# Attention over banded and dilated keys: turning the probability tiles beyond eight through one PSUM bank, interleaved with the other eight

## The reference, cut to what matters

```python
# window: query block n (128 queries) sees blocks n-1, n, n+1 and 256 context keys
p = softmax(concat([q @ k_local + mask, q @ k_context, sink]))
y = p_local @ v_local + p_context @ v_context
# grid: rows of 64, a query sees 8 rows x 16 columns around it, plus the context, with a bias
p = softmax(concat([q @ k_local + bias, q @ k_context]))
# dilated: causal, three dilations (128,1), (512,4), (2048,16), mixed by their softmax sums
y = sum(w[c] * (softmax(q @ k[c]) @ v[c]) for c in range(3))
```

## Time and profile before

| what | value |
|---|---|
| executions | 2537.91, 2540.40, 3635.32 us (median 2540.4) |
| profiled execution | 2537.63 us |
| its span, first to last instruction | 2535.7 us |
| PE busy of the span | 98% |
| DVE busy | 60% |
| ACT busy | 31% |
| mean granted TensorE clock | 0.995 of full |

### The profile page before, as it was taken

How to read it: one execution, slowest core, us unless ns; L and a number is a source line. 1 busy time by engine, 2 the same in 40 slices (tenths; PEclk the granted TensorE clock), 3 DMA queues, 4 the chain that set the end, 5 groups by cost and what they waited for, 6 DMA issues and landing times.

```text
span 2535.7 us, 38631 instructions
## 1 busy us (share of the span) xinstructions
PE 2472.3 (98%) x14777; PEld 1820.8 (72%) x14777; DVE 1508.9 (60%) x3740; ACT 784.9 (31%) x1752; POOL 299.9 (12%) x487
## 2 busy tenths in 40 slices
PE   6999999999999999999999999999999999999999
PEld 3477688777788685566788776868578866546867
DVE  2358776699866663443453477757868684514554
ACT  2237511277721123332210066113312274121210
POOL 1101100000051000000043022310000002222000
PEclk9999999999999999999999999999999999999999
DMA  7031000022033221311001011523240105334321
GB/s 276 21 108 52 23 34 34 34 76 80 14 100 108 68 98 44 104 41 43 9 23 43 34 50 44 104 100 117 83 150 34 67 27 142 115 108 174 126 97 52
DMA packets 75096, 193.69 MB, mean 76 GB/s; under 512 B 7821, under 2 KB 10577, under 8 KB 73985
## 3 DMA queue, kind: packets, MB, share of 16 engines
q0 software_dynamic: 28688, 99.67, 12.6%
q1 hardware_dynamic: 45472, 91.16, 10.3%
q10 hardware_dynamic: 752, 0.38, 0.1%
HBM read 149.46 MB, written 42.07 MB: 76 GB/s over the span
## 4 chain that ended last, share of the span: by engine, by line
PE 92%; DVE 3%; ACT 2%; issue 2%; DMA 1%; ACTq 0%; DVEq 0%; POOL 0%
PE psum L1586 37%; PE psum L1950 11%; PE psum L1890 7%; PE psum L1993 5%; PE psum L1990 5%; PE psum L2083 4%; PE psum L1974 3%; PE psum L1967 3%; PE psum L1700 3%; PE psum L1811 3%; PE psum L1572 1%; PE psum L1553 1%; PE psum L2154 1%; PE psum L2172 1%; PE psum L2141 1%
## 5 line engine op out<-in xcount | busy, mean ns | idle before, releaser
L3546 ACT ACTIVATE RP<-RP,small 128x1280 f32<-128x1280 f32 (+11 forms) x274 | 252.8, 923 | 154.8 <-DVE small L3056 154.5
L1950 PE MATMUL psum<-RQ 64*128 64x256 f32 (+5 forms) x1344 | 293.3, 492 | 2.0 <-DVE small L3056 1.2
L3056 DVE CUSTOM_DVE_ANT_0 RP<-psum,small 128x512 f32<-128x512 f32 (+1 forms) x382 | 201.8, 574 | 107.4 <-PE psum L1974 86.5
L1890 PE MATMUL psum<-RW,hT 128*128 128x512 f32 (+3 forms) x608 | 217.1, 512 | 1.0 <-ACT hT L3275 1.0
L1950 PEld LDWEIGHTS psum<-RQ 64*128 64x128 f32 (+1 forms) x1344 | 148.4, 191 | 72.0 <-issue 41.5
L1890 PEld LDWEIGHTS psum<-RW,hT 128*128 128x128 f32 x608 | 128.5, 216 | 75.1 <-issue 57.4
L1586 PE MATMUL psum<-RW,hT 128*128 128x256 f32 x736 | 167.0, 379 | 0.0
L1993 PE MATMUL psum<-RQ,RP 128*128 128x128 f32 x1312 | 159.8, 276 | 0.5 <-ACT YR L3580 0.5
L1993 PEld LDWEIGHTS psum<-RQ,RP 128*128 128x128 f32 x1312 | 152.1, 192 | 5.3 <-issue 4.6
L1586 PEld LDWEIGHTS psum<-RW,hT 128*128 128x128 f32 x736 | 139.6, 190 | 21.7 <-issue 2.2
L1586 PE MATMUL psum<-RW,RP 128*128 128x256 f32 x576 | 136.1, 379 | 0.0
(11 more groups left out here) (545 smaller groups left out, 4275.0 us busy)
## 6 DMA issues: line engine op xcount, KB each, us to landing
RW<-in_w_in SPq DMA_DIRECT2D x7, 2048.0 KB, 7.8
RW<-in_od_w_ada SPq DMA_DIRECT2D x6, 2048.0 KB, 8.1
RW<-in_ev_w_in SPq DMA_DIRECT2D x5, 2048.0 KB, 7.8
RW<-in_od_w_in SPq DMA_DIRECT2D x5, 2048.0 KB, 7.9
RQ<-in_ev_w_ada SPq DMA_DIRECT2D x4, 2048.0 KB, 19.6
RX<-in_x POOLq DMA_DIRECT2D x12, 512.0 KB, 7.8
RW<-in_ev_w_ada SPq DMA_DIRECT2D x2, 2048.0 KB, 8.7
RW<-in_ev_w_out SPq DMA_DIRECT2D x2, 2048.0 KB, 8.5
```

The source lines that it names most:

```text
L1890: last = pe.matmul(main.bank(f)[:, c0:c0 + nc_], lhs_of(st["lhs"], j["t"], kk), w, start=kk == 0, stop=kk == kn - 1)
L1950: last = pe.matmul(main.bank(f)[:, 0:pc["w"]], q, kk[:, keys], start=i == 0, stop=i == len(u["qk"]) - 1)
L3056: drained(main, dve.tensor_tensor_reduce(pair_slot(st, u, lane)[:, pc["at"]:pc["at"] + pc["w"]], main.bank(f)[:, 0:pc["w"]], add, -scale, ...
L3546: fn(pr, pr, ACT.Exp, bias=mins[:, at, lane, n - 1:n], scale=-1.0, accum_out=total).then_inc(s_pexp, 1)
```

## The change

It touches only the three stages named above.

1. A unit with 9 to 12 tiles is "woven": its rest (2 or 4 tiles) takes one fill of `main` instead of two, and both halves of a tile land side by side in it, 128 columns a tile. These are 24 units of window, 24 of grid (10 tiles) and 8 of dilated (10 tiles at t=4, 12 at t=5): 56.
2. PE turns a woven unit in a new order (`turn_woven`). At each step a half 0 and a half 1 are issued together: halves 0 of the rest, then of the eight; halves 1 of the eight, then of the rest. So the array's upper side writes the rest's bank at the start and its lower side at the end, and in between a wait of PE on its own semaphore (`s_woven`, "excess_first_halves_turned") stands. All banks are waited for at the start.
3. The rest of a woven unit is copied out by one engine, all of it and in one piece: by ACT in even units, by DVE in odd ones. It was copied by both, a half each.
4. DVE's and ACT's copies go in the opposite order in all units: the eight first, then the rest (`u["turns"][::-1]`). This holds for the units of dilated at t=6 and t=7 too (14 and 16 tiles), which are not woven and keep two fills for the rest; PE's order there stays as it was, rest first.
5. In `turn`, a woven unit's fill for DVE is numbered ahead of that for ACT.

```diff
@@ planner @@
                         if c == n - 1:
-                            ch["halves"] = [turn.new("act"), turn.new("dve")]
-                            ch["f"] = ch["halves"][1]
+                            woven = n == 2 and len(tiles) <= 12
+                            if woven:
+                                second, first = turn.new("dve"), turn.new("act")
+                                ch["halves"], ch["f"] = [first, second], first
+                            else:
+                                ch["halves"] = [turn.new("act"), turn.new("dve")]
+                                ch["f"] = ch["halves"][1]
...
+                if kind in ACROSS and woven:
+                    woven_count[0] += 1
+                    u["woven"], u["turned"] = woven_count[0], [u["turns"]] * 2
...
                     for ch in u["turns"][:-1]:
-                        ch["halves"] = [main.new("act"), main.new("dve")]
-                        ch["f"] = ch["halves"][1]
+                        if len(ch["tiles"]) <= 4:
+                            ch["f"] = main.new("dve" if at % 2 else "act")
+                        else:
+                            ch["halves"] = [main.new("act"), main.new("dve")]
+                            ch["f"] = ch["halves"][1]
@@ PE @@
+                    def turn_woven(u):
+                        rest, eight = u["turns"]
+                        pe.wait_ge(s_pexp, 2 * u["g"] + 2)
+                        for ch in (rest, eight):
+                            for f in ch.get("halves", [ch["f"]]):
+                                ch["ring"].wait_free(pe, f)
+                        r = len(rest["tiles"])
+                        first, second = eight["halves"]
+                        whole = main.bank(rest["f"])
...
+                        for at in range(r + 8):
+                            if at < r:
+                                ins = turn_half(at, 0, whole[:, P * at:P * at + HD])
+                                if at == r - 1:
+                                    ins.then_inc(s_woven, 1)
+                            else:
+                                last = turn_half(at, 0, turn.bank(first)[:, HD * (at - r):HD * (at - r) + HD])
+                            if at < 8:
+                                other = turn_half(r + at, 1, turn.bank(second)[:, HD * at:HD * at + HD])
+                            else:
+                                if at == 8:
+                                    pe.wait_ge(s_woven, u["woven"])
+                                other = turn_half(at - 8, 1, whole[:, P * (at - 8) + HD:P * (at - 8) + P])
+                            if at == 7:
+                                turn.written(other)
+                        turn.written(last)
+                        main.written(other)
...
-                            for ch in u["turns"]:
-                                turn_chunk(u, ch)
+                            if "woven" in u:
+                                turn_woven(u)
+                            else:
+                                for ch in u["turns"]:
+                                    turn_chunk(u, ch)
@@ DVE (ACT has the same with side "act") @@
+                            if k in ACROSS and "halves" not in ch:
+                                if ring.side[ch["f"]] == "dve":
+                                    ring.wait_full(dve, ch["f"])
+                                    if ch["c"] >= 4:
+                                        dve.wait_ge(s_chunk, ch["c"] - 2)
+                                    n = len(ch["tiles"]) * P
+                                    drained(ring, dve.tensor_copy(pair_turned(ch["c"])[:, 0:n], ring.bank(ch["f"])[:, 0:n]), ch["f"])
+                                continue
...
-                            turned_chunks(u, u["turns"])
+                            turned_chunks(u, u["turns"][::-1])
```

More of the change, by code:

```diff
@@ L177, in build @@
         divided = [0]
+        woven_count = [0]
         main = Ring(psum, [0, 1, 2, 3, 4], sem("main_full"), {"act": sem("main_read_act"), "dve": sem("main_read_dve")})
@@ L217, in build @@
         s_rec = sem("pair_reciprocals_ready")
+        s_woven = sem("excess_first_halves_turned")
         s_gated = sem("columns_gated")
@@ L1953, in scores, with turn_half @@
                                         main.written(last)
+                    def turn_woven(u):
[7 more added lines that the diff above has]
+                        whole = main.bank(rest["f"])
+                        def turn_half(at, half, dst):
+                            lane, key, _ = (rest["tiles"] + eight["tiles"])[at]
+                            rows = slice(HD * half, HD * half + HD)
+                            return pe.transpose(dst, pair_slot(st, u, lane)[rows, key:key + P], ident[rows, rows])
+                        for at in range(r + 8):
[15 more added lines that the diff above has]
+                        main.written(other)
                     def turn_chunk(u, ch):
@@ L1960, in turn_chunk @@
                         ring = ch["ring"]
-                        if k in ACROSS:
+                        if "halves" in ch:
                             for f in ch["halves"]:
@@ L3551, in turned_chunks @@
                             ring = ch["ring"]
+                            if k in ACROSS and "halves" not in ch:
+                                if ring.side[ch["f"]] == "act":
+                                    ring.wait_full(act, ch["f"])
+                                    if ch["c"] >= 4:
+                                        act.wait_ge(s_chunk, ch["c"] - 2)
+                                    n = len(ch["tiles"]) * P
+                                    ring.consumed(fn(pair_turned(ch["c"])[:, 0:n], ring.bank(ch["f"])[:, 0:n], ACT.Copy), ch["f"])
+                                continue
                             if k in ACROSS:
```

## The result

The changed kernel takes 2546.66 us (median of 13 executions, 2541.26 to 2548.99), the kernel before 2538.16 (13 executions in the same session). The ratio is 1.0031, with a 95% interval of 1.0023 to 1.0040; one execution of the kernel before, of 3635.32 us, is left out of it. The forecast was 2544, and the measured time lies inside its range of 2536 to 2552.

What follows compares the result with a forecast made beforehand. PE bounds the kernel, busy 98%, with late copies able to become its wait. Window 0.2, grid 0.3, woven dilated 0, t=6 and t=7 2.6, last units 2.2 sum to +5.3 us on 2538.6: forecast 2544, range 2536 to 2552.

Steps and rivals of the forecast that it cites:

- t=6 and t=7 with scores behind them: Dilated: fourth score fill waits for ACT's later copy of the rest; 0.4 us four times, 0.5 twice, together 2.6.
- The last two units: Dilated's end, t=7: values start at 2.70 instead of 1.59 us after the turn; +1.11 twice, 2.2 us.
- Window, +0.2: Window stage: pairs stay about level (6.45 against 6.46 us); once, short next-but-one scores make the rest late, +0.2 us.
- with the 0.05 from above, values at 2.04: Even window units: values follow ACT's copy of the rest by 0.05 us, 0.13 late, unit 3.28 us.
- Grid, +0.3 and otherwise nothing: Grid stage: the last ten-tile unit, no scores ahead of its values, loses 0.3 us; row ends and other units zero.
- Woven dilated units, 0: Dilated stage: the eight woven units come out at zero by the same steps as window.
- The weave itself, 0: Woven units: PE's twenty transposes in two alternating sides stay the same work, and the weave costs nothing.
- the wait may just touch: Four twelve-tile units: PE's own wait names step 3, 0.32 us before, and might barely cost something.
- rival B: Woven units: PE's wait on its own semaphore drains the array, 56 x 0.17 = 9.5 us more, 2553.5; chance 0.15.
- A: Woven units gain because the rest's copy is never last: -4 instead of +0.5 us, 2539.5 in all; chance 0.27.
- C: Dilated's end: PE's busy time falls to about 2.3 of 3.40 us and the clock drops, 2547; chance 0.13.
- D: The change does not do what it says; dismissed since main's fills are five a unit in PE's list.

Runs made afterwards that it cites:

- e1: Changed kernel, but the unwoven units at t=6 and t=7 copy the rest first again, the old order: 2540.37 us, ratio 1.0003.
- e4: Changed kernel with PE's wait on its own semaphore moved to one step behind the transpose it waits for: 2558.78 us, ratio 1.0080.
- e11: Changed kernel with PE's wait on its own semaphore three steps behind the transpose it waits for: 2552.70 us, ratio 1.0056.
- e8: Changed kernel, rest's halves 1 turned midway, rest copied first and by DVE, old copy order everywhere, old fill numbering: 2536.40 us, ratio 0.9991.
- e7: Kernel before, nothing woven, DVE alone copies both fills of the rest where it has at most 4 tiles: 2535.83 us, ratio 0.9984.
- e6: Changed kernel with DVE copying the rest in all woven units and the old copy order at t=6 and t=7: 2536.95 us, ratio 0.9993.
- e5: Changed kernel, but ACT copies the rest in all woven units: 2547.29 us, ratio 1.0032.

## Why the prediction was right, and where it was off

The sum was +5.3 us; the turns of the two traces, counted from one to the next, give the following.

- **t=6 and t=7 with scores behind them:** 0.4 four times and 0.5 twice, 2.6. From the first turn at t=6 to the first at t=7 it was 17.47 us and is 19.21, +1.74; the next two units took 9.64 and take 10.67, +1.03. Together 2.8. Right, mechanism and size: at t=6 and at t=7 the load of the fourth fill goes at 2.16 and 2.40 after the turn, forecast 2.16 and 2.39, and e1 confirms it by undoing it.
- **The last two units:** +1.11 each, values at 2.70. Measured 1.10 and 2.69. Right.
- **Window, +0.2:** off. The copy order, the start of the rest's copy (1.61 forecast, 1.62) and the odd unit (3.17) were right, but the even unit takes 3.38, not 3.28. The step that was mis-sized is "with the 0.05 from above, values at 2.04": the 0.05 was the time from an ACT copy's end to the load of a score fill, put where values follow a copy. Values follow ACT's copy by 0.11 here, as they follow DVE's by 0.12, and the twenty loads take 1.10 instead of 1.07. The pair rose by 0.09 instead of falling by 0.01: about 1 us over twelve pairs. A window unit with a piece of modulation (from 202.55 us before) gave half of that back: it went from 5.58 to 5.08 us, since its fourth score fill, which had gone at 1.80 after the turn (204.35), no longer waits.
- **Grid, +0.3 and otherwise nothing:** the last unit's 0.3 measured 0.36. The step "units at the rows' ends stand beside ones with larger waits now, and I take zero" failed: the first three rows take 0.41, 0.26 and 0.26 us more, 0.9 together. The last ten-tile unit of a row gives 0.20 of it each time: it went from one turn to the next in 2.93 us and now takes 3.13, because its values could start early and the rest isn't there. I had named the loss and set it off against a gain in the other units. In the second row, whose units are like those of the rows behind it, the five ten-tile units ahead of the last one changed by -0.11, +0.08, -0.03, +0.11 and -0.03, so there was no gain to set against it. The fourth row's 0.40 is the last unit's 0.36 and 0.04 elsewhere, so the stage costs 1.3 in all.
- **Woven dilated units, 0:** the four at t=4 took 13.40 us and take 13.48, the four at t=5 15.23 and 15.67: +0.5. Most of it is the first unit at t=5, an even one (3.70 to 4.09), whose values' load stands 0.68 us instead of 0.33 and whose first matmul names ACT's copy of the rest.
- **The weave itself, 0:** right. The twenty loads take 0.70 us as before (0.84 us for the transposes), no gap stands ahead of the last ones, and e4, e11 and e8 show how near the wait would have to come to cost something: under five steps. The twelve-tile units, of which the prediction said that the wait may just touch, have it at five: their loads take 0.84 us instead of 0.82 to 0.83. The Trainium skill ("TensorEngine Tiling (Array Packing)", Key Properties) says that only a change of tiling mode drains TensorE, not a change of tile, and by it the 9.5 us of rival B were zero; these runs agree, with 0.84 us for the woven turn of twenty as for the one in order.

2.8 + 2.2 from the exchanged order, 0.5 from window, 1.3 from grid, 0.5 from dilated: 7.3, where the ratio gives 8, with 2 us of uncertainty. The prediction had 5.3 of it. What it lacks are the woven units: the 0.1 us by which their values in even units come later or take longer than forecast, and the last units of grid's rows, taken as zero. That the total is near comes from the exchanged order, which was right; of the woven stages it had 0.5 of 2.3.

**The rivals.** A (the woven units gain, 2539.5) fell: "ACT is late, not short of time" was the argument against it, and the rest's copy by ACT is last in every second unit. A had counted on 4 us less from the woven units. From turn to turn e7 (nothing woven, DVE copies the rest first) has 4.6 and e8 (woven, the same) 3.2; e6, where DVE copies it but last, has 0.8. So the gain was there to be had, with the rest copied first and by DVE. B (the weave's wait drains the array) fell with the loads of 0.70 us, and e4 and e11 show what such a wait costs where it does. C (the clock falls at dilated's end) fell too. The end of dilated, columns as in the earlier trace rows:

```profile
2116.80:2120.20 3.40, 1.90 (x46) 1.62 (x44) 1.63 (x4) 2.71 (x6) 0.00 (x0) 1.00 0.00 0
...
2123.60:2127.00 3.40, 2.30 (x36) 2.16 (x37) 1.41 (x3) 1.01 (x4) 0.00 (x0) 1.00 0.00 0
```

PE is busy for 1.90 and 2.30 of 3.40 us there, as little as the 2.3 forecast or less, and the granted clock stays at 1.00, the 2.4 GHz level. A fall behind a stretch with 1.69 of 3.40 didn't mean one here. D was never in question: the scores are all alike, which is what the change says.

**What stays open.** Why the twenty loads of the values take 1.10 instead of 1.07 us was not tried. It is not the order of copies by itself: in e5 the rest is copied last in every unit, and the loads take 1.07 in the units that don't wait for it and 1.10 in those that do. Nor was why the load of a score fill follows its copy in 0.05 us and that of the values in 0.11; the two differ in more than one thing, and I have only rows for it. The numbering of `turn`'s fills (point 5 of the change) was never tried alone.

## What to carry to other kernels

Before a ring of banks is made shorter in fills, look at who reads the fill that is late: moving one small copy a unit to the engine that stood idle just then gave 4 us with a few changed lines (e7). The rebuilt order of transposes with everything repaired gave no more (e6 and e8, ratios of 0.9993 and 0.9991, against 0.9984). An exchanged order of copies has to be priced in every unit that runs through the same loop, above all in those at the end of a stage that have nothing ahead of their values; there it cost 1.10 us a unit and no gain stood against it. And profile the kernel before twice: two profiles of it differ by 3.2 us at their ends, two fifths of the effect that was to be explained.

## What the runs showed of the hardware that was not expected

- A wait of PE on its own semaphore in a running stream costs what is left of about 0.31 to 0.33 us after the instruction that it names: one step of 0.063 us behind it 0.25 us (e4), three steps 0.14 (e11), four steps about 0.07 (e8, twelve tiles, 0.90 against 0.82 to 0.84), seven steps nothing (loads of a turn 0.70 us).
- Values follow the end of a copy by ACT in 0.11 us (224.31 to 224.42), that of a score fill by 0.05. A handoff read at one place of the list isn't good for another.
- A list that is the same in all units can run with period two: 3.14 and 3.41 us in turn (e5). Behind a unit in which PE waited, ACT's exponential started before the turn, behind one without a wait after it.
